# Projection in rounded products, rank sums on the matrix engine, first gates copied on chip

## What is computed

```python
h  = rmsnorm(x, norm1_g) * (1 + sc1) + sh1
q, k, v, f = split_in(h, w_in)
att  = diff_attention(q, k, v, lam)          # 4 heads, two softmax maps each
four = fourier_mix(f, w_fourier)             # Re(FFT2) per group, then 128x128
x  = x + g1 * (concat(rmsnorm(att) * (1 - lam_init), four) @ w_out)
h2 = rmsnorm(x, norm2_g) * (1 + sc2) + sh2
q  = h2 @ w_query                            # 8 heads, two halves of 128
s1, i1 = top_k(q[..., 0] @ keys0, 16); s2, i2 = top_k(q[..., 1] @ keys1, 16)
top, pos = top_k(s1 + s2 (all pairs), 16)    # an expert is i1 * 128 + i2
x  = x + g2 * sum_k softmax(top)_k * gelu(u[idx_k] . h2) * v[idx_k]
y  = rmsnorm(x, final_g)
```

## Time and profile before

| | us |
|---|---|
| median of 3 runs (lowest, highest) | 1818.26 (1815.53, 1819.26) |
| the profiled execution | 1815.94 |
| its span, first to last instruction | 1813.9 |
| PE busy | 1665.3 |
| DVE busy | 1506.1 |
| POOL busy | 916.1 |
| ACT busy | 645.6 |
| mean granted TensorE clock | 0.966 of full |

### The profile page before, as it was taken

The page is one execution under the profiler, slowest core; times in us unless marked ns, Lnnn a source line. Parts: engine busy times, 40 slices in busy tenths (PEclk is TensorE's granted clock), DMA queues, the critical chain, the costliest instruction groups (busy, mean ns, idle before and its releaser), DMA issues.

```text
span 1813.9 us, 28223 instructions
## 1 busy us (share of the span) xinstructions
PE 1665.3 (92%) x9322; PEld 1442.0 (79%) x9338; DVE 1506.1 (83%) x3069; ACT 645.6 (36%) x1085; POOL 916.1 (51%) x771
## 2 busy tenths in 40 slices
PE   4999998999954886899999999999999999999994
PEld 2776766479953886799999999999999999999993
DVE  0732266457999999799999999999999999999997
ACT  1212266121103785233333333333333333333331
POOL 1101000013402665777778877777666666666661
PEclk9999999999976998999999999999999999999997
DMA  9445202140010668999999999999999999999993
GB/s 355 173 163 208 75 1 98 42 184 3 1 47 1 187 186 253 385 406 409 407 408 390 402 409 409 409 409 409 409 408 409 409 409 403 410 409 407 406 397 124
DMA packets 198137, 518.28 MB, mean 286 GB/s; under 512 B 14643, under 2 KB 64435, under 8 KB 197941
## 3 DMA queue, kind: packets, MB, share of 16 engines
q0 software_dynamic: 73728, 268.47, 37.3%
q1 hardware_dynamic: 122320, 245.59, 36.3%
q10 hardware_dynamic: 2022, 3.38, 0.5%
HBM read 486.45 MB, written 30.93 MB: 285 GB/s over the span
## 4 chain that ended last, share of the span: by engine, by line
PE 79%; DVE 10%; DMA 5%; issue 3%; ACT 3%; POOL 0%; SPq 0%; POOLq 0%; ACTq 0%; DVEq 0%; PEldq 0%; another core or an unknown queue 0%
PE ps L1786 20%; PE ps L1785 20%; PE ps L1784 19%; PE ps L1758 4%; PE ps L1873 4%; DMA arena_w<-in_w_mod 2%; PE ps L1599 2%; PE ps L1603 2%; PE ps L1600 2%; PE ps L1697 2%; DMA arena_w<-in_w_in 1%; ACT arena_w L867 1%; DVE arena L1470 1%; PE ps L1721 1%; DVE arena L1307 1%
## 5 line engine op out<-in xcount | busy, mean ns | idle before, releaser
L1786 PE MATMUL ps<-hT_hi,U_lo 128*128 128x384 f32 x1024 | 344.3, 336 | 0.0
L1784 PE MATMUL ps<-hT_hi,U_hi 128*128 128x384 f32 x1024 | 344.1, 336 | 0.0
L1785 PE MATMUL ps<-hT_lo,U_hi 128*128 128x384 f32 x1024 | 343.5, 335 | 0.0
L537 POOL DMA_INDIRECT rows_under<-in_expert_u,idxn x192 | 273.8, 1426 | 116.4 <-issue 41.8
L1784 PE MATMUL ps<-hT_hi,C_hi 128*128 128x512 f32 x768 | 301.2, 392 | 14.5 <-DVE C_lo L1447 14.5
L537 POOL DMA_INDIRECT rows_under<-in_expert_v,idxn x192 | 242.7, 1264 | 140.4 <-DVE arena L1470 77.8
L1786 PE MATMUL ps<-hT_hi,C_lo 128*128 128x512 f32 x768 | 303.2, 395 | 0.0
L1785 PE MATMUL ps<-hT_lo,C_hi 128*128 128x512 f32 x768 | 303.1, 395 | 0.0
L1470 DVE SCALAR_TENSOR_TENSOR arena<-rows_under,dots,arena 128x1024 f32<-128x1024 f32 x192 | 247.8, 1291 | 4.8
L930 ACT ACTIVATE act_t<-ps 128x384 f32<-128x384 f32 x128 | 63.0, 492 | 386.2 <-PE ps L1786 386.2
L1784 PEld LDWEIGHTS ps<-hT_hi,U_hi 128*128 128x128 f32 x1024 | 192.6, 188 | 4.9
(11 more groups left out here) (273 smaller groups left out, 3010.9 us busy)
## 6 DMA issues: line engine op xcount, KB each, us to landing
U_in<-in_expert_uT SPq DMA_DIRECT2D x128, 512.0 KB, 8.7
arena<-in_expert_v SPq DMA_DIRECT2D x128, 512.0 KB, 6.5
arena_w<-in_w_mod SPq DMA_DIRECT2D x12, 2048.0 KB, 12.4
gate_in<-gates_scratch SPq DMA_DIRECT2D x62, 384.0 KB, 7.9
gates_scratch<-arena_w SPq DMA_DIRECT2D x5, 4096.0 KB, 16.6
arena_w<-in_w_in SPq DMA_DIRECT2D x4, 2048.0 KB, 8.7
arena_w<-in_w_query SPq DMA_DIRECT2D x4, 2048.0 KB, 10.8
arena_w<-in_w_out SPq DMA_DIRECT2D x2, 2048.0 KB, 8.4
```

The costliest lines, as they stand in the source:

```text
L537: pool.indirect_dma_start(out=rowr[row], out_offset=None, in_=table, in_offset=bass.IndirectOffsetOnAxis(ap=idxn[:, g, row:row + 1], axis= ...
L1784: nc.tensor.matmul(out, hi, rhi, start=start, stop=False)
L1785: nc.tensor.matmul(out, hi, rlo, start=False, stop=False)
L1786: return nc.tensor.matmul(out, lo, rhi, start=False, stop=stop)
```

## The change

It makes no difference in what is computed, apart from the rounding of the projection. (1) The projection is made of three rounded products, first all blocks with the first half of `w_out`, then with the second, each block's second half followed by the transposes of the block before. The high and low parts of the mixed tokens (`mix_hi`, `mix_lo`) and of `w_out` are made before: ACT and DVE in Fourier stage and attention, POOL `out_low`. POOL instead of DVE makes the low part of the first quarter of `w_query`. (2) The sums over ranks of the first four blocks are 16 accumulating matmuls per half (`pick`); ACT `key_squares` writes the key and its square. (3) The gates of the third dense block for the first two pairs are copied by ACT from `gbuf` to `gate_in`, the others loaded a little earlier. (4) Turn 0 handles no gathered rows; the prompt's selection is done there; turns 1 to 16, now written out, take 17 rows each.

Not shown below: new semaphores, other places of buffers, `mix_low` for the small units, the order of the `w_query` slots. Code of the engines is indented less than in the file.

```diff
-    jobs = []
-    for o in order:
-        if isinstance(o, tuple):
-            jobs.append((o, "dve"))
-        else:
-            kind = "merge" if o[0] == "m" else "h2T"
-            jobs += [((kind, int(o[1]), half), "dve") for half in range(2)]
+    jobs = [(("merge", b, 0), "dve") for b in range(NBLK)]
+    for b in range(NBLK):
+        jobs.append((("merge", b, 1), "dve"))
+        jobs += [(("h2T", b - 1, half), "dve") for half in range(2 if b else 0)]
+    jobs += [(("h2T", NBLK - 1, half), "dve") for half in range(2)]
     return jobs
...
         H2.append(cutout(CO + 14336, D))
-        mixT = cutout(WO + WRING * KD * NC, 5120).rearrange("p (k t) -> p k t", k=KD)
+        mix_hi = HT_lo
+        mix_lo = HT_hi[:, :, :].rearrange("p k t -> p (k t)").rearrange("p (b k t) -> p b k t", b=NBLK, k=KD)
+        wo_hi = [w_lo[:, DFT_C % WRING], wq_lo_first[:, :, :]]
+        wo_lo = [w_lo[:, (OUT_C + half) % WRING] for half in range(OUT_CH)]
+        half_sum = cutout(CO + 14336, D).rearrange("p (r n) -> p r n", r=2)
...
 sp.wait_ge(s_wT, len(UNITS))
 for b in range(NBLK):
     sp.dma_start(X[:, b], xall[b * P:(b + 1) * P, :]).then_inc(s_xr[b], 16)
-sp.wait_ge(s_mix, NBLK)
 sp.wait_ge(s_out, 32)
+sp.wait_ge(s_fill2, NBLK)
 sp.dma_start(wq_in[0], w_query_v[:, :, 0:NC]).then_inc(s_wq[0], 16)
 for b in range(NBLK):
-    sp.wait_ge(s_x1, 2 * (b + 1))
+    sp.wait_ge(s_x1, NBLK + b + 1)
     sp.dma_start(x1_d[b * P:(b + 1) * P, :], X[:, b]).then_inc(s_spill, 16)
...
 sp.wait_ge(s_spill, 16 * NBLK)
+sp.wait_ge(s_gtop, 2)
 at = [GCUT[1] // 2] + [2 * NBLK + 3 * b for b in range(NBLK + 1)] + [TWICE]
 for b in range(NBLK + 1):
...
+def out_low(half):
+    src = chunk[:, (OUT_C + half) % WRING]
+    for k in range(KD):
+        pool.wait_ge(s_ohi, KD * half + k + 1)
+        pool.tensor_tensor(wo_lo[half][:, k, :], src[:, k, :], wo_hi[half][:, k, :].bitcast(f32),
+                           ALU.subtract).then_inc(s_olo, 1)
+def query_low(ci, ks):
+    for k in ks:
+        pool.wait_ge(s_qhi, KD * ci + k + 1)
+        pool.tensor_tensor(wq_lo[ci][:, k, :], wq_in[ci][:, k, :], wq_hi[ci][:, k, :].bitcast(f32),
+                           ALU.subtract).then_inc(s_qlop, 1)
+out_low(0)
 for b in range(NBLK):
     pool.wait_ge(s_avar, b + 1)
     pool.tensor_tensor(ss4[:, 1, :], ss4[:, 0, :], powe[:, 0:H], ALU.pow).then_inc(s_arstd, 1)
+out_low(1)
 for b in range(NBLK):
+    if b == NBLK - 1:
+        query_low(0, range(2 * b - 2, 2 * b))
     pool.wait_ge(s_var2, b + 1)
     pool.tensor_tensor(rstd[:, b:b + 1], ss[:, b:b + 1], powe[:, 0:1], ALU.pow).then_inc(s_rstd2, 1)
+    if 0 < b < NBLK - 1:
+        query_low(0, range(2 * b - 2, 2 * b))
...
         pool.wait_ge(s_gout[0], 16 * NDEN)
+        pool.wait_ge(s_gtop, 2)
     if first and row == 2:
-        for part in s_gin:
-            pool.wait_ge(part, 16)
+        pool.wait_ge(s_gpart[0], 16)
     if first and row == 6:
         pool.wait_ge(s_gq, QUADS * NDEN)
...
+def out_high(half, ks):
+    i = OUT_C + half
+    act.wait_ge(s_chunk[i % WRING], 16 * (i // WRING + 1))
+    for k in ks:
+        act.copy(wo_hi[half][:, k, :], chunk[:, i % WRING, k, :]).then_inc(s_ohi, 1)
 act.wait_ge(s_lam, 1)
 act.wait_ge(s_bc, 4 * MOD_CH)
+act.wait_ge(s_chunk_used, DFT_C + 1)
 exps(0)
 for i in range(len(UNITS) + 6):
...
 def square2(b):
-    act.wait_ge(s_x1, 2 * (b + 1))
+    act.wait_ge(s_x1, NBLK + b + 1)
     act.activation(H2[b], X[:, b], ACT.Square, accum_out=ss[:, b:b + 1]).then_inc(s_sq2, 1)
...
+def key_squares(n):
+    act.wait_ge(s_picked, 2 * n + 2)
+    if n:
+        act.wait_ge(s_stackfill, n)
+        act.wait_ge(s_key2, n)
+    act.copy(key2[:, 0, :], ps[:, 0, 256:384]).then_inc(s_keysq0, 1)
+    act.activation(square, ps[:, 0, 256:384], ACT.Square).then_inc(s_keysq0, 1)
+    act.wait_ge(s_keysq0, 2 * n + 2)
+    act.copy(key2[:, 1, :], square).then_inc(s_keysq, 1)
 def stack_out(b):
     act.wait_ge(s_stackfill, b)
...
     if b == NDEN and p == 18:
         split_v(0, 0, 1, True)
+    if b == NDEN and p == QUADS - 4:
+        act.wait_ge(s_diff, QUADS * NDEN)
+        for g in range(2):
+            act.dma_start(gate_in[:, g, 0:4 * P].rearrange("p (c n) -> p c n", c=4),
+                          gates_d[g, :, 0:4].rearrange("p c e t -> p c (e t)")).then_inc(s_gin[g], 16)
+act.wait_ge(s_gev, QUADS * NDEN)
+for g in range(2):
+    act.copy(gate_in[:, g, 4 * P:6 * P].rearrange("p (c e t) -> p c e t", c=2, e=2),
+             gbuf[:, :, 2 * g:2 * g + 2, :]).then_inc(s_gtop, 1)
 share_exps(NDEN + 1)
...
-act.wait_ge(s_gout[0], 16 * NDEN)
-act.wait_ge(s_gout[1], 16 * (NDEN - 1))
-act.wait_ge(s_gpart[0], 16)
-for g in range(2):
-    act.dma_start(gate_in[:, g], gates_d[g].rearrange("p c e t -> p (c e t)")).then_inc(s_gin[g], 16)
 experts(0, True, False)
...
+def mix_low(u):
+    s, g = u
+    src = bank1("fmix", s, g)
+    dve.wait_ge(s_fhi, units.index(u) + 1)
+    if s == 0:
+        dve.tensor_tensor(mix_lo[:, 0, 4 + g, :], src[:, 0:P], mix_hi[:, 4 + g, 0:P].bitcast(f32),
+                          ALU.subtract).then_inc(s_dve1, 1)
+    else:
...
+def att_low(b):
+    dve.wait_ge(s_mix, b + 1)
+    dve.scalar_tensor_tensor(out=mix_lo[:, b, 0:4, :], in0=ps[:, 7, :].rearrange("p (h t) -> p h t", h=H),
+                             scalar=lam[:, 7:8], in1=mix_hi[:, 0:4, b * P:(b + 1) * P].bitcast(f32),
+                             op0=ALU.mult, op1=ALU.subtract).then_inc(s_mixlo, 1)
...
     src = bank2("merge", b, half)
-    dve.tensor_tensor(H2[b][:, cols], src, M[:, c, G1, cols], ALU.mult).then_inc(s_dve2, 1)
+    part = H2[b][:, cols] if half else half_sum[:, b % 2]
+    dve.tensor_tensor(part, src, M[:, c, G1, cols], ALU.mult).then_inc(s_dve2, 1)
     dve.wait_ge(s_dve2, B2.emptied(B2.pos[("merge", b, half)])[1])
-    dve.tensor_tensor(X[:, b, cols], X[:, b, cols], H2[b][:, cols], ALU.add).then_inc(s_x1, 1)
+    dve.tensor_tensor(X[:, b, cols], X[:, b, cols], part, ALU.add).then_inc(s_x1, 1)
 def turned_low(b):
...
-turned_low(4)
+dve.wait_ge(s_out, 32)
+for b in range(NBLK):
+    merge(b, 0)
+for b in range(NBLK):
+    merge(b, 1)
+    var2(b)
+    if b:
+        turned_low(b - 1)
+    make_h2(b)
+turned_low(NBLK - 1)
...
+def picked(n, ws, bd=0, share=(0, 0, 0, 0)):
+    b = ORDER[n]
+    for w in ws:
         gate_quads(bd, share[2 * w])
+        onehot = onehots[w if n < LATE_PICK else 0]
         o4 = onehot.rearrange("p j (s h) -> p j s h", h=PH)
+        if n and n < LATE_PICK:
+            dve.wait_ge(s_picked, 2 * n - 1 + w)
+        elif n >= LATE_PICK and w == 0:
+            dve.wait_ge(s_picked, 2 * LATE_PICK)
         link(dve.tensor_tensor(o4, spread(ranks[:, w, :]).unsqueeze(1).broadcast_to([P, TOPK, TOPK, PH]),
                                places[:, :, :].unsqueeze(2).broadcast_to([P, TOPK, TOPK, PH]), ALU.is_equal))
-        eqs = note(dve.tensor_tensor(o4, o4, idxf[:, w].unsqueeze(2).broadcast_to([P, TOPK, TOPK, PH]), ALU.mult))
-        gate_quads(bd, share[2 * w + 1])
-        dve.wait_ge(s_step, eqs)
+        eqs = dve.tensor_tensor(o4, o4, idxf[:, w].unsqueeze(2).broadcast_to([P, TOPK, TOPK, PH]), ALU.mult)
+        if n < LATE_PICK:
+            eqs.then_inc(s_eqs, 1)
+            gate_quads(bd, share[2 * w + 1])
+            continue
+        link(eqs)
         for n_ in (8, 4, 2):
             link(dve.tensor_tensor(onehot[:, 0:n_], onehot[:, 0:n_], onehot[:, n_:2 * n_], ALU.add))
         link(dve.tensor_tensor(sel[:, w, :].rearrange("p (h s) -> p s h", h=PH), spread(onehot[:, 0]),
...
+def choice_rows(n, first, second):
+    dve.scalar_tensor_tensor(out=idx[:, SPARSE.index(ORDER[n]), :], in0=first, scalar=float(NKEY), in1=second,
+                             op0=ALU.mult, op1=ALU.add).then_inc(s_idx, 1)
+def finish(n):
     if n < NDEN:
-        dve.tensor_copy(key2[:, 0, :], sel[:, 1, :])
-        link(dve.tensor_tensor(square, sel[:, 1, :], sel[:, 1, :], ALU.mult))
-        link(dve.tensor_copy(key2[:, 1, :], square))
+        dve.wait_ge(s_keysq, n + 1)
         dve.tensor_tensor(key2[:, 2, :], square, key2[:, 1, :], ALU.subtract).then_inc(s_key2, 1)
-    if b in SPARSE:
-        dve.scalar_tensor_tensor(out=idx[:, SPARSE.index(b), :], in0=sel[:, 0, :], scalar=float(NKEY), in1=sel[:, 1, :],
-                                 op0=ALU.mult, op1=ALU.add).then_inc(s_idx, 1)
+    elif n < LATE_PICK:
+        dve.wait_ge(s_picked, 2 * n + 2)
+        dve.tensor_copy(sel[:, 1, :].rearrange("p (h j) -> p h j", h=PH), spread(ps[:, 0, 256:384]).rearrange("p j h -> p h j"))
+        dve.wait_ge(s_step, note(dve.tensor_copy(sel[:, 0, :].rearrange("p (h j) -> p h j", h=PH),
+                                                 spread(ps[:, 0, 384:512]).rearrange("p j h -> p h j"))))
+        choice_rows(n, sel[:, 0, :], sel[:, 1, :])
 def gate_weights(n):
...
+    if n == 1:
+        finish(0)
     gate_quads(bd, pairs_share)
     pair_first(n, 3)
     gate_quads(bd, pairs_share)
...
     pair_second(n, 3)
     pair_last(n, 3)
...
```

(81 more changed lines are left out.)

173 lines of the change are left out of this document (85 added, 88 removed).

## The result

The changed kernel takes **1825.04 us** (median of 7 runs, 1822.92 to 1826.17), the kernel before 1818.43 (7 runs beside it): ratio 1.0036, 95% interval 1.0025 to 1.0048. It is 6.6 us slower where I forecast 16.5 faster. The profiled execution took 1826.17 us, span 1824.3, which is 10.4 above the span of before.

A forecast was written before the change was run, and what follows sets the result against it. It took TensorE to bound the projection, VectorE to lead the gate stage, and experts to run 8.307 us per block with DMA near its limit. Sum: 0 + 0.5 - 8 - 12 + 3 = -16.5, say 1801.5 us, range 1785 to 1815.

The forecast's parts named there:

- Projection stage, 67 us: Projection by three rounded products: stage takes 67 us instead of 74.9, a gain of 8.
- Preparation, 7.7 longer: Ahead of the projection: low halves and casts on VectorE, ScalarE and GpSimd lengthen the time by 7.7 us.
- Collision with GpSimd in the search, plus or minus 3: Query and key stages: the 4.14 us VectorE wait for GpSimd falls on another pass, plus or minus 3 us.
- Choice of block 0, +0.5: Block 0's rank sums on TensorE at its lower clock: a loss of 0.5 us (-1.5 to +3).
- Gate stage, gain 8: Next three blocks' rank sums: VectorE sheds 12 us, TensorE takes 12.5; stage 131.5 us, gain 8 (0 to 12).
- Start of the experts, gain 12: Expert start without gathered rows: 17.6 us earlier at block 3, less a 5.5 us stall for U block 4.
- Catching up, +3 (0 to 13): Expert turns 1 to 16 with 17 rows: DMA needs 418 GB/s, gives 409; loss 3 us (0 to 13).
- written-out turns were taken as 0: Expert turns 1 to 16, unrolled: loading their code was taken to cost 0 us.
- Rival C: Expert turns: DMA gives under 397 GB/s to 17 rows a turn, so the kernel is slower, 1836 at 385; 6%.
- Rivals A: Whole kernel: everything is hidden, gates gain 12, the start 17.6, no DMA limit; 1782 us, chance 15%.
- B: Gate stage: TensorE becomes the bound, picks take back all VectorE sheds, projection nets +3; 1813 us, chance 15%.
- D: Expert start: first products still wait, now for U, so the start gains 4 only; 1810 us, chance 10%.

The follow-up runs named there:

- after_again: The changed kernel unaltered, run again as the measure for other kernels of its call; 1824.1 us, ratio 1.0043 to the kernel before.
- unrolled: The kernel before with VectorE's turns 1 to 16 written out instead of looped, nothing else; 1820.4 us, ratio 1.0019.
- r16_act: r16_gather with the 3.67 MB rest of the last gate store issued by ScalarE instead of SyncE; 1811.2 us, ratio 0.9957 to the kernel before.
- r16_gather: r16 with gathers of rows 1 to 5 no longer waiting for ScalarE's gate copies or the store's first part, row 0 sixth; 1808.1 us, ratio 0.9946.
- r16: The changed kernel with 16 gathered rows again in turn 0, no 17-row turns, loops, block 0's choice before turn 0; 1813.1 us, ratio 0.9971 to before.

## Why the prediction was wrong, point by point

**Projection stage, 67 us: right**, 67.5. **Preparation, 7.7 longer: right in size, in part by luck**, 7.1 to the first merge. Attention is 6.7 of it in this profile and 3.3 in that of after_again. Nor is it right item by item: in the profile the loss sits in the first eight units and beside a low clock, and the four low-half passes that I charged with 1.5 cost nothing visible in the later units (40.4 us from the ninth unit to the last exponential, as before). Net of both -0.3, forecast 0.

**Collision with GpSimd in the search, plus or minus 3:** nothing, the search ends 0.3 us earlier as everything does.

**Choice of block 0, +0.5: wrong by 2.7**, it gained 2.2. The term was mis-sized, the 32 rank-sum matmuls: I took 0.26 us each from the dense products at the lower clock, where the first 16 took 1.86 in all, at the same granted clock of 0.50, and ran beside VectorE's second products (kernel after, TensorE):

```profile
558.75 1.86 PE L1973 MATMUL ps<-arena 128*128 128x128 bf16 x16 [23.69 <-DVE arena L1425]
561.05 1.89 PE L1976 MATMUL ps<-arena 128*128 128x128 bf16 x16 [0.44 <-DVE arena L1425]
```

The nearest row had the shape but not the type: these are bf16 on both sides. In the gate stage, at the full clock, 16 took 1.06 us (TensorE's timeline, kernel after), so that the picks cost some 6.4 us there and not the 12.5 I charged:

```profile
634.88 1.06 PE L1973 MATMUL ps<-arena 128*128 128x128 bf16 x16
```

**Gate stage, gain 8: wrong**, 2.8. The working took VectorE's 131 us for the bound and asked only whether TensorE's sum of busy time would replace it. What failed in it is "TensorE's 119.7 + 12.5 = 132", which takes busy time for all that the stage needs. VectorE did shed 10.8 us (131.0 to 120.3), and the stage came out at 136.5 with TensorE busy for 122.7, so neither load alone bounds it; which hand-over does isn't shown. The pace of the quads stood just behind VectorE: 96 quads at 1.35 us are 130, and start and end come on top.

**Start of the experts, gain 12: nearly right to block 3**, 11.9 (from -5.3 to -17.2). The stall is there at the place and with the cause I gave, U block 4 behind the store, 6.3 us of TensorE against 5.5. Its mechanism was another: I let the load be issued at 716 and queue in the DMA engines, but SyncE couldn't issue it before 724.8. At block 4, behind the wait and the low clock, 8.8 are left.

**Catching up, +3 (0 to 13): this is the step that failed.** It measured 19.9. The sum of bytes was about right, and so was the rate later (407 against the 409 that I put in). What was wrong is the sentence "235 MB are due; at 340 for the first 8.9 and 409 after": it lets DMA run full from 717 on. It couldn't. With no row used in turn 0, eight buffers took eight gathers (the eighth waited for block 0's weights until 735), and DMA ran at 302 and then 323 GB/s until 785. I had named the eight rows waiting at turn 1 as an argument in favour, where they were the limit. 16 rows put off are 20.6 us of a full DMA. In bytes: by 785 the sentence has 8.9 MB and 51 us at 409 GB/s, 29.8 MB, and the windows from 705 on give 25.0. The missing 4.8 MB alone are 11.8 us. The sentence is also off in its own sum: 708 + 26 + 226.1 MB at 409 GB/s is 1287 and not 1289, so the term should have been +1.

A second, smaller step failed beside it: written-out turns were taken as 0. 17.0 of the 19.9 us lie in the turns of 17 rows; of the 2.9 behind them unrolled, which puts no row off, shows 1.8. By the times of unrolled the written-out turns cost 1 to 6 us.

**Rival C** (DMA has no reserve) had the right resource with the wrong trigger: it needed DMA to fall under 397 GB/s with 17 rows. It gave 407, as it did to the kernel before, and the loss came all the same. The Trainium skill ("HBM Reference", the note under the opening table) gives about 425 GB/s for a core streaming alone. By it 17 rows, 418 GB/s, would have fitted. None of the windows of the expert stage shown here, of 10 to 575 us, is above 409, and the measurement decides.

**Sum.** To block 4 the change gained 14.1 in the profile, where the steps forecast 19.5; behind it stand +19.9 instead of +3, and 4.6 us that no step had: later turns of 16 rows (1.8, as much as unrolled loses there) and a late VectorE at the end (2.8). Rivals A, B and D, like the forecast, foresaw a gain; none has turn 0 leave DMA idle.

## What to carry to other kernels

Where a transfer engine runs within 2% of its rate for a thousand microseconds, its idle time at the start is the only reserve there is: before work is put off to "catch up", write down the bytes moved by a fixed time in both versions, with the number of buffers as a limit, and not just the rate needed later. An earlier start of the computing engine is worth only what DMA also does earlier. And look at what stands in a queue behind a transfer of thousands of small packets: on the queue of an engine that issues nothing next it holds no load. That this saves time by itself isn't shown here (r16_act 1811.2, r16_gather 1808.1).

## What the hardware showed that I had not expected

- A DMA issue can hold the issuing engine for long: 14.18, 22.43 and, for the same load in r16, 10.74 us behind the 3.67 MB store of 512-byte packets, against 0.33 us usually. Cut into pieces it held less, up to 2.2 us behind single pieces and up to 9.09 behind two, but later loads landed late. On ScalarE's queue it took 0.46 us to issue, and V block 3 0.33.
- DMA gave 407 GB/s over 575 us both to turns that asked for 402 (16 rows) and to turns that asked for 418 (17 rows).
- 16 accumulating bf16 matmuls of 128x128 took 1.9 us at a granted clock of 0.50, 0.12 each, half of what the dense products take there.
- The length of TensorE's low clock at the start of attention differs between profiles of the same code: 10.2, 13.7, 17.1 and 23.9 us, with attention 65.9 to 69.3 us long.
